# Dilated layer: where its heads and its output projection stand among the projections

## The reference, cut to what matters

```python
h = x @ b_w_in                                    # 1024 -> 18*128 dilated queries + 4*64 memory queries
qd = h[..., :2304].reshape(B, S, 3, 6, 128)       # three groups (window, dilation) of six heads
kv = (x @ shared_w_kv)                            # 6 keys and 6 values of 128
mix = _dilated_attention(qd, shared_k, shared_v)  # per head: three masked score matrices, one softmax over all
mo = _mem_attn(qm, mkv_k, mkv_v)                  # 4 heads of 64 over 256 memory rows
y = concatenate([mix, mo]) @ w_out[l]             # 1024 -> 1024
x = layer_norm(ALPHA * x + y)
```

## Time and profile before

| | us |
|---|---|
| median of three runs | 2760.17 (2748.7 to 2790.65) |
| the profiled execution | 2751.64, its span 2750.0 |
| dilated stage, first projection to last output matmul | 984.4 to 1142.1 |
| PE busy over the span | 2659.9 (97%) |
| DVE, ACT, POOL busy | 1886.9, 1339.9, 156.4 |
| mean granted clock of PE | 0.989 of full speed |

### The profile page before, as it was taken

The page is one execution under the profiler, slowest core; times in us unless marked ns, Lnnn a source line. Parts: engine busy times, 40 slices in busy tenths (PEclk is TensorE's granted clock), DMA queues, the critical chain, the costliest instruction groups (busy, mean ns, idle before and its releaser), DMA issues.

```text
span 2750.0 us, 42954 instructions
## 1 busy us (share of the span) xinstructions
PE 2659.9 (97%) x17035; PEld 2357.2 (86%) x17035; DVE 1886.9 (69%) x3592; ACT 1339.9 (49%) x2155; POOL 156.4 (6%) x135
## 2 busy tenths in 40 slices
PE   7999999999999999999999999999999899899997
PEld 7889999998888888799999988888787778787776
DVE  5667888965555655769789655556766669556588
ACT  4434554445554534446444454455335457363465
POOL 0006100000000001043000000000011000000000
PEclk9999999999999999999999999999999999999999
DMA  6354544455555644445544555556531569423486
GB/s 223 93 196 140 180 162 154 158 180 191 193 192 194 225 163 139 133 140 183 163 160 154 174 188 194 195 192 208 176 125 25 173 226 355 164 78 94 165 302 233
DMA packets 175415, 480.04 MB, mean 175 GB/s; under 512 B 27232, under 2 KB 43504, under 8 KB 175216
## 3 DMA queue, kind: packets, MB, share of 16 engines
q1 hardware_dynamic: 172048, 474.34, 51.4%
q10 hardware_dynamic: 3168, 2.97, 0.4%
HBM read 475.67 MB, written 1.57 MB: 174 GB/s over the span
## 4 chain that ended last, share of the span: by engine, by line
PE 84%; issue 9%; DVE 5%; ACT 2%; POOL 1%; DMA 0%; ACTq 0%; POOLq 0%; SPq 0%; DVEq 0%
PE ps L135 82%; PE ps L138 1%; DVE big L163 1%; DVE spl L155 1%; DVE st L183 1%; DVE xb L163 0%; ACT big L141 0%; ACT spl L141 0%; POOL big L155 0%; DVE big L155 0%; DVE xr L155 0%; ACT xr L141 0%; DMA ring<-in_w_mem_kv_dram 0%; ACT L141 0%; POOL st L155 0%
## 5 line engine op out<-in xcount | busy, mean ns | idle before, releaser
L141 ACT ACTIVATE whi<-ring 128x1024 fp32r<-128x1024 f32 x512 | 543.0, 1061 | 679.6 <-PE ps L135 679.4
L155 DVE TENSOR_TENSOR ring_rest<-ring,whi 128x1024 fp32r<-128x1024 f32 x468 | 572.1, 1223 | 347.2 <-ACT whi L141 347.1
L135 PE MATMUL ps<-xr,whi 128*128 128x256 f32 x4096 | 745.8, 284 | 0.5 <-ACT big L141 0.4
L135 PEld LDWEIGHTS ps<-xr,whi 128*128 128x128 f32 x4096 | 637.6, 192 | 1.4 <-ACT big L141 1.3
L135 PE MATMUL ps<-whi,Ar 128*128 128x512 f32 x2048 | 630.8, 389 | 0.0
L135 PE MATMUL ps<-xr,ring_rest 128*128 128x256 f32 x2048 | 579.1, 283 | 0.0
L155 DVE TENSOR_TENSOR spl<-ring,spl 128x1024 fp32r<-128x1024 f32 (+3 forms) x384 | 435.4, 1163 | 103.4 <-ACT spl L141 93.3
L135 PEld LDWEIGHTS ps<-whi,Ar 128*128 128x128 f32 x2048 | 384.4, 188 | 79.8
L141 ACT ACTIVATE spl<-ring 128x1024 fp32r<-128x1024 f32 (+3 forms) x384 | 373.3, 1008 | 87.6 <-PE ps L135 76.0
L135 PE MATMUL ps<-ring_rest,Ar 128*128 128x512 f32 x1024 | 398.4, 389 | 0.0
L135 PEld LDWEIGHTS ps<-xr,ring_rest 128*128 128x128 f32 x2048 | 392.6, 192 | 0.0
(11 more groups left out here) (135 smaller groups left out, 2323.5 us busy)
## 6 DMA issues: line engine op xcount, KB each, us to landing
ring<-in_peer_u_dram SPq DMA_DIRECT2D x256, 512.0 KB, 3.5
ring<-in_peer_v_dram SPq DMA_DIRECT2D x256, 512.0 KB, 3.5
ring<-in_moe_gate_up_dram SPq DMA_DIRECT2D x128, 512.0 KB, 5.1
ring<-in_moe_w_down_dram SPq DMA_DIRECT2D x64, 512.0 KB, 5.2
ring<-in_peer_w_q_dram SPq DMA_DIRECT2D x32, 512.0 KB, 5.0
ring<-in_sb_w_in_dram SPq DMA_DIRECT2D x24, 512.0 KB, 4.6
ring<-in_ab_w_in_dram SPq DMA_DIRECT2D x20, 512.0 KB, 5.8
ring<-in_w_out_dram SPq DMA_DIRECT2D x16, 512.0 KB, 4.6
```

The costliest lines, as they stand in the source:

```text
L135: return self.e.matmul(o, l, r, start=start, stop=stop)
L141: return self.e.activation(o, i, f, **k)
L155: return self.e.tensor_tensor(o, a, b, op)
```

## The change

The memory query projection Bm moves to the second place, with banks 4 and 5; all other projections of the stage stand in banks 0 to 3. The 14 steps of the memory heads run at two places per unit in units 4 to 10, the first three steps of the dilated heads in units 17, 18 and 19. Nine dilated steps follow alone, then steps 12 to 17 among the halves of the output projection. Its quarters come in the order 3 (memory), 0, 1, 2, each turned when its heads are stored. Both barriers, all 20 fillers and the stage's own bank plan go.

```diff
@@ heads_step_pe: before the output product
+                need(pe, j.get("then", ()))
@@ finish
+            elif stage == "dil":
+                dil_finish(e, name, following)
@@
-        out_units("wo1", io["w_out"][1], 0, 1, 2, 3)
+        out_units("wo1", io["w_out"][1], 3, 0, 1, 2)
@@ projB: Bm behind Bq0
+            if n0 == 0:
+                projB.append(projection("Bm", WB, 2304, 256, ...))
+        for p_, b_ in zip(projB, (0, 4, 0, 0, 0, 0, 0, 0, 0, 0)):
+            p_["base"] = b_
@@ jobsB: each job waits for its own queries, keys and values
+                    after=stored(projB, *[q_at(6 * g + h) for g in range(3)], k_at(h)),
+                    then=stored(projB, *[(8 + h // 4, k) for k in range(t + 1)]),
+        jobsM = mem_jobs(1, qmT1, stored(projB, (1, 0), (1, 1)), 768)
+        planM = beside_plan(jobsM)
+        buffersM = heads_buffers(13696, 256, 32)
+        M_AT = [(4 + s // 2, 2 * (s % 2)) for s in range(14)]
+        D_AT = [(17, 0), (18, 0), (19, 0)]
+        planB = {("scores", 0): 4, ("scores", 1): 5, ("scores", 2): 7}
+        next_bank = 2
+        for s in range(3, 17):
+            for kind, i, n in (("out", s-5, 1), ("turn", s-3, 1), ("scores", s, (total(jobsB[s % 12]) + 511) // 512)):
+                if not 0 <= i < 12:
+                    continue
+                if s >= 12:
+                    planB[kind, i] = 6 if kind == "out" else 4 + s % 2
+                    continue
+                next_bank = next_bank if next_bank + n <= 7 else 0
+                planB[kind, i] = next_bank
+                next_bank = (next_bank + n) % 7
+        def dil_beside(e): ...      # memory steps at M_AT, dilated steps 0 to 2 at D_AT
+        def dil_middle(e):
+            for s in range(3, 12):
+                dil_step(e, s)
+                if s in (3, 4) and e.name == "A":
+                    round_half(e, ("wo1", 0), s - 3)
+                elif s in (3, 4) and e.name == "V":
+                    rest_half(e, ("wo1", 0), s - 3)
+                if s == 5:
+                    dil_turn(e, 0)
+            dil_turn(e, 1)
+        def dil_finish(e, name, following):
+            for s in range(12, 18):
+                dil_step(e, s)
+                if s == 15:
+                    dil_turn(e, 2)
+                if s < 17:
+                    out_half(e, name, (s - 12) // 2, s % 2, following)
+            out_half(e, name, 2, 1, following)
+            dil_turn(e, 3)
+            out_both(e, name, 3, following)
@@ dil_pe (dil_act, dil_dve and dil_pool alike)
-            project_all(pe, projB, "x2")
-            psum.close(("end", "B"))
-            busy(pe, 4)
-            join(pe, "B")
-            pe.wait_ge(arrival("kv1"), 16)
-            heads_pe(pe, "dil", jobsB, planB, PTB, PmB, 2, 0)
-            psum.close(("end", "dil"))
+            project_all(pe, projB, "x2", 0, None, dil_beside(pe))
+            dil_middle(pe)
```

More of the change, by code:

```diff
@@ L702, in heads_pool, with heads_buffers @@
                         *gps.next((name, "sum", i)))
-        def heads_buffers(base, W):
+        def heads_buffers(base, W, st0=0):
             def Sm(i):
@@ L714, in stat @@
             def stat(i):
-                return st[:, 4 * (i % 8):4 * (i % 8) + 4]
+                return st[:, st0 + 4 * (i % 8):st0 + 4 * (i % 8) + 4]
             return PT, Pm, Sm, stat
@@ L1793, in build @@
             projB.append(projection(f"Bq{n0}", WB, 128 * n0, 128 * k, [Tcols(128 * i, 128, qD[:, n0 + i, :]) for i in range(k)]))
-        projB += [projection("Bm", WB, 2304, 256, [Tcols(128 * i, 128, qmT1[:, i, :]) for i in range(2)]),
-                  projection("Bk", WK, 0, 512, [Tcols(128 * i, 128, kD[:, i, :]) for i in range(4)]),
+            if n0 == 0:
+                projB.append(projection("Bm", WB, 2304, 256, [Tcols(128 * i, 128, qmT1[:, i, :]) for i in range(2)]))
+        projB += [projection("Bk", WK, 0, 512, [Tcols(128 * i, 128, kD[:, i, :]) for i in range(4)]),
                   projection("Bl", WK, 512, 256, [Tcols(128 * i, 128, kD[:, 4 + i, :]) for i in range(2)]),
@@ L1798, in build, with q_at, k_at @@
                   projection("Bw", WK, 1280, 256, Nrows(0, 256, lambda t: vD[:, t, 512:768]))]
+        for p_, b_ in zip(projB, (0, 4, 0, 0, 0, 0, 0, 0, 0, 0)):
+            p_["base"] = b_
+        def q_at(n):
+            return ((0, 2, 3, 4, 5)[n // 4], n % 4)
+        def k_at(h):
+            return (6 + h // 4, h % 4)
         jobsB = []
@@ L1808, in build @@
                     sum=3, vs=[vD[:, k, 128 * h:128 * h + 128] for k in range(t + 1)],
+                    after=stored(projB, *[q_at(6 * g + h) for g in range(3)], k_at(h)),
+                    then=stored(projB, *[(8 + h // 4, k) for k in range(t + 1)]),
                     store=lambda dve, pv, r, dst=dst: dve.tensor_scalar(dst, pv, r, None, ALU.mult)))
-        jobsB += mem_jobs(1, qmT1, (), 768)
-        planB = bank_plan(jobsB, [0])
-        PTB, PmB, SmB, statB = heads_buffers(8192, 768)
@@ new lines, in build @@
+        D_AT = [(17, 0), (18, 0), (19, 0)]
+        planB = {("scores", 0): 4, ("scores", 1): 5, ("scores", 2): 7}
+        next_bank = 2
+        for s in range(3, 17):
+            for kind, i, n in (("out", s - 5, 1), ("turn", s - 3, 1), ("scores", s, (total(jobsB[s % 12]) + 511) // 512)):
+                if not 0 <= i < 12:
[6 more added lines that the diff above has]
+                next_bank = (next_bank + n) % 7
@@ new lines, in build, with dil_step, dil_beside, beside @@
+        buffersB = heads_buffers(8192, 768)
+        def dil_step(e, s):
+            heads_step(e, "dil", jobsB, planB, buffersB, s)
+        def dil_beside(e):
+            def beside(i, k):
+                if (i, k) in M_AT:
+                    if (i, k) == M_AT[0] and e.name == "P":
+                        e.wait_ge(arrival("kv1"), 16)
+                    heads_step(e, "memB", jobsM, planM, buffersM, M_AT.index((i, k)))
+                if (i, k) in D_AT:
+                    if (i, k) == D_AT[1] and e.name == "V":
+                        for t in range(2):
+                            e.wait_ge(arrival(f"dil{t}"), 16)
+                    dil_step(e, D_AT.index((i, k)))
+            return beside
@@ new lines, in dil_turn @@
+        def dil_turn(e, k):
+            marks = ((vec, ("memB", "stored", 7)), (vec, ("dil", "stored", 3)), (vec, ("dil", "stored", 7)), (vec, ("dil", "stored", 11)))
+            out_turn(e, "wo1", k, [marks[k]], 7)
+        def dil_middle(e):
[8 more added lines that the diff above has]
+            dil_turn(e, 1)
@@ L1828, in dil_act @@
             act.dma_start(kvm[1], kept).then_inc(arrival("kv1"), 16)
[L1829 to L1833, removed]
-        def dil_dve(dve):
[L1836 to L1842, removed]
+            project_all(act, projB, "x2", 2, None, dil_beside(act))
+            dil_middle(act)
+        def dil_dve(dve):
+            project_all(dve, projB, "x2", 2, None, dil_beside(dve))
+            dil_middle(dve)
         def dil_pool(pool):
[L1845 to L1848, removed]
+            heads_pool(pool, "dil", jobsB, buffersB[1])
         pr = scr[:, 0:5680].rearrange("p (t n) -> p t n", t=2)
```

## The result

The changed kernel takes 2762.26 us, the median of 20 runs (2756.99 to 2789.99), the kernel before 2751.86 (20 runs, 2748.7 to 2790.65). The ratio is 1.0044, 95% interval 1.0026 to 1.0062: a slowdown of about 10 us, small but clear of noise, and far inside 2%. A second set of runs of the same two kernels says the same: 2763.05 us (10 runs) against 2752.45 (29 runs), ratio 1.0036 (1.0014 to 1.0058).

What follows compares the result with a forecast made beforehand. The prediction took PE, 84% of the span, as the bound. Its parts, 21.4 + 21.1 + 26.2 = 68.7 us against 62.8, made it 5.9 us slower: 2762 us, between 2757.5 and 2766.1, range 2747 to 2783.

Steps and rivals of the forecast that it cites:

- five bank waits: Among the projections, PE waits for ACT's copy of the last output out of a reused bank: 4.9 us.
- three DVE waits: Memory steps at units 6, 8 and 10: PE waits for a bank DVE must free, together 3.3 us.
- the wait on `xr`: Output projection: PE waits on the last quarter's turn with nothing left to put beside it, 1.8 us.
- What can be gained at most: Dilated stage after the last projection: removing barriers, fillers and waits can bring at most 10.8 us.
- Part 1: Projections: moved heads and new bank and DVE waits add 21.4 us before the last projection ends.
- Part 2: Dilated steps 3 to 11, from the last projection to the first output half: 21.1 us, against 14.4 of PE work.
- T + 3.4: Transposes of dilated job 1 start 3.4 us after the last projection ends, with PE waiting 1.9 us.
- rounding and rests: First two dilated cycles: two roundings on ACT and two rests on DVE delay the heads by 1.8 us.
- the memory quarter's turn: First two dilated cycles: turning the memory quarter on ACT and DVE delays the heads by 0.6 us.
- The clock: Granted clock stays 1.00; a rival had it fall in steps 3 to 11, +20 us in all, chance 0.05.
- Part 3: Output projection with the remaining dilated work and turns: PE always has work until the last turn's wait, sum 26.2 us.
- faster: the waits are hidden: Rival: DVE and ACT waits vanish in the projections and steps 3 to 11, -4.1 us; gain over 1 us, chance 0.20.

Runs made afterwards that it cites:

- e9: The changed kernel profiled again without any edit: stage 171.34 us at clock 1.00, against 173.06 in its first profile; median 2763.05 us.
- e1: The changed kernel with other banks for projections Bk (4 to 7) and Bv (2 and 3): stage 168.92 us.
- e6: The kernel before with all projections of the stage in banks 0 to 3: stage 170.17 us, against 164.31.
- e2: The changed kernel with every memory step one place later in its unit: stage 166.77 us.
- e4: The changed kernel with the first output weights split beside the last projections, not between dilated steps 3 to 5: stage 170.40 us.
- e3: The changed kernel with the last quarter's turn one output half earlier: stage 170.93 us.
- e8: The changed kernel with other banks for Bk and Bv, later memory steps, early-split output weights and an earlier last turn: stage 162.92 us, median 2751.4.
- e12: Changed kernel with new banks, later memory steps, early weight splitting, four dilated steps beside projections, quarter 0 turned after step 10, banks taken late: stage 163.18 us, median 2749.92.
- e11: The changed kernel with PE taking each projection bank right before its first matmul, in all stages: stage 171.31 us with the clock falling to 0.50.
- e7: The kernel before without the 20 fillers of the dilated stage: stage 172.74 us with the clock near half, median 2752.89 us, ratio 1.0001.

## Why the prediction was right, and where its terms were off

Direction, time (2762 us forecast, 2762.26 measured) and mechanism held. The agreement of the time is partly luck: I had placed it between the profiled run and a median of three runs that lay 8.3 us above the median of twenty, and the slowdown itself was forecast at 5.9 us and came out at 8.75 in the stage, 7.0 with the clock at 1.00, and 10.4 in the medians, just past the "2 to 10 us slower" of the forecast. All the signs named for it came (five bank waits, of which the trace names ACT as releaser for two, three DVE waits, the wait before the first POOL-released transposes, over 19 us to the first output matmul, the wait on `xr`), except the clock of 1.00.

- **What can be gained at most, 10.8 us.** Right in kind: in the stage PE's busy time fell by 1.7 us (159.55 to 157.90 in e9), less than the 4.3 us of fillers that went, and its idle time rose by 8.7 (4.8 to 13.4). Only waits and fillers were traded.
- **Part 1, 21.4 us.** 1100.51 (the end of the row at 1099.07, 12 x 0.12) less the start of the stage, which is 0.28 earlier than before, makes 21.5. Bank waits are 0.92, 0.93, 0.75, 0.72 and 1.03, sum 4.35 for 4.9; e1 and e6 show their cause. DVE waits 0.90, 0.75 and 1.43, sum 3.1 for 3.3; e2 shows that the place makes them. What is left, the heads, is 14.0 for 13.2: their own rows are 12.7, and each switch from a projection's matmuls to a head's costs 0.06 to 0.19 us that I did not count, 1.3 in all.
- **Part 2, 21.1 us.** 1123.70 - 1100.51 = 23.2, and 21.5 in e9. The start, T + 3.4, was at T + 3.3. The first output half's bank wait was as forecast. The terms inside were mis-sized against each other: rounding and rests 0.9 for 1.8 (e4), the memory quarter's turn about 1.9 for 0.6 (rows of e4). Together 2.9 for 2.4, so that the sum came out better than its terms.
- **The clock.** The step that failed: "My longest wait is 1.9 us, like the 1.69 of the gla stage", from which I kept 1.00 and put the fall at 0.05 with 20 us. It does fall, in some executions, but for about 3 us and at a price of 1.7; the 20 us took the whole middle at 1.2 GHz. The length of the longest wait does not tell it: the fall came behind 1.68 us and several shorter waits, and with the same waits in e9 it did not come. What decides it is not shown. By the rule that I cited from the Trainium skill ("TensorE: Matmul & The Clock Gate", "A second HAM failure mode: psum-queue depth-cycling") the clock swings under frequent short idles between groups of matmuls. This trace agrees in kind, with 0.50 in one window, but e9, the same kernel, stayed at 1.00, and so did five of the six kernels with one edit to it.
- **Part 3, 26.2 us.** 1150.78 - 1123.70 = 27.1. The last turn's wait was 1.7 for 1.8. Not foreseen: 0.42 us (0.56 from start to start) before job 11's output product, which shares bank 6 with the product before it, and DVE is late with that one's store. e3 shows in addition that PE's end is not what ends the stage.
- **The rival "faster: the waits are hidden"** is out as it was put. It takes other places and banks to hide them, and then it does come in the stage (162.92 in e8, 163.18 in e12, against 164.31); in the whole kernel it is not clear of the noise.
- **What stays open.** The medians differ by 10.4 us, the stage by 7.0 to 8.75. The third layer's stage, the same code in all kernels but e11 and e12, took 168.52 us in the changed kernel's profile and 166.82 before, but over the fourteen profiles it goes from 163.86 (e2) to 196.44 (e6), 174.11 in e9. The granted clock goes with it: between 2080 and 2120 it is 0.50 in e6, 1.00 before and after the change. So two executions can lie 30 us apart by that stage alone. Whether the change shifts how often it takes longer was not settled. The second PEER stage takes a constant 0.25 us more (813.15 to 813.19 for 812.9) in nine profiles of the changed kernel and its variants; this wasn't looked into.

## What to carry to other kernels

Putting work "beside" a busy engine does not shorten what that engine must do; the gain is bounded by its idle time and fillers, and new waits come out of the same purse. Before moving such work, look for two things at each place: whether the PSUM bank there was just written and still has a reader, and whether the engine that must free it has other work queued ahead. One place later (4.6 us) and another set of banks (2.4) are together worth the 7.0 us that the change had cost, each measured alone. And look at which engine ends a stage: a wait taken from PE came back in the norm, where DVE was the last.

## What the runs showed of the hardware

- Where PE takes a bank whose last output ACT has still to copy, it costs 0.84 us on average (e6: seven places, six copies of 256 columns and one of 512, 5.9 us more), though the copy of 256 columns itself takes 0.38 us.
- The granted clock can fall to 0.50 in a stage where no idle stretch of PE is longer than 1.7 us, in two of eight profiled executions (changed, e11), and is back at 1.00 after 3 to 4 us; in e7 it stayed near half for over 14 us. The same kernel can be profiled with the fall (changed, 173.06) and without it (e9, 171.34).
- With the clock at 1.00, ten fillers in idle time cost nothing that could be measured (171.40 against 171.34).
